# Four input tiles' low parts made ahead of the second projection chunk's low weights, on VectorE

## The chip, the cores and the metric

The kernel runs on one core of a Trainium2 chip. The metric is the device time of one execution in microseconds (us); before the change the median of three runs is 1078.63 us. TensorE multiplies, VectorE (DVE) and ScalarE (ACT) do the elementwise work, and SyncE (SP) issues the transfers from memory.

## The reference

Two transformer blocks over 256 tokens of width 1024, in float32: first an attention block with a gated linear-attention half and a convolved feed-forward part, then a two-layer block (an RWKV-7 layer and a latent-attention layer). Only the start of the first block matters here:

```python
mod = jax.nn.silu(c) @ w_ada[l] + b_ada[l]
shift1, scale1, gate1, shift2, scale2, gate2 = jnp.split(mod, N_MOD, axis=-1)
h = modulate(rms_norm(x, g_norm1[l]), shift1, scale1)      # h * (1 + scale) + shift
proj = h @ w_in[l]                                         # 1024 -> 3088 columns
sb_q, sb_k, sb_v, gq, gk, gv, gg, gf = jnp.split(proj, offsets, axis=-1)
```

`proj` then feeds the stick-breaking attention (`sb_q`, `sb_k`, `sb_v`) and the gated linear attention.

## The kernel before

**Split operands.** Each large product is made in float32 precision from three products of rounded operands. An operand v is split into a high part (v rounded by a copy) and a low part (v minus the high part); then w·x = w_hi·x_hi + w_lo·x_hi + w_hi·x_lo. For weights, ScalarE makes the high part (`act_split`, line 306) and VectorE the low part (`dve_split`, line 321). For the input h of the projection, which lies in SBUF as eight tiles of 128x256 (`kt` 0 to 7), ScalarE makes `h_hi` (line 987), and VectorE scales and shifts the tile in place in `ub` (line 1059) and subtracts (`h_lo`, line 1062).

**Weight stream.** All weights come in chunks of at most 128x2048, in one fixed order, through four buffers (`raw`), issued by SyncE. Before it issues chunk n, SyncE waits until chunk n-4 has been used up: for a split chunk that is VectorE's low part (`lo_made`), for a chunk of `w_ada` it is VectorE's weighted sum (`ada_done`). `w_ada` is not split: ScalarE makes the first two of eight products with c (line 528), VectorE the other six (line 556) and a last sum (line 562), and TensorE sums over the partitions with tiny matmuls (line 572). The order around the change is w_in 0, w_in 2, ada 8, w_in 4, ada 9, w_in 7, ada 10, w_gf, ada 11, w_in 8, ada 12, w_in 9 and so on. With split chunks counted from 0, w_in 0 is chunk 0, w_in 2 chunk 1, w_in 4 chunk 2, w_in 7 chunk 3, w_gf chunk 4 and w_in 8 chunk 5.

**Order of the engines.** Each engine has its own program, written out by hand, and works it off in order; semaphores tie them together. VectorE's program of this part is `dve_one`: after the last `w_ada` chunk of the start it makes the norm's gain (line 1053), then the low weights of chunks 0 and 1 (lines 1055 and 1056), then the eight pairs of lines 1059 and 1062, then `ada` 8 and the low weights of chunk 2, and from there one step for each chunk c: evacuation, an `ada` chunk, a split, and pieces of the attention. ScalarE's program makes the high weights of chunk 0, the eight `h_hi`, the high weights of chunk 1, two copies out of a bank, its part of ada 8, and the high weights of chunk 2; then it waits for the end of chunk 0 on TensorE (line 684).

TensorE multiplies chunks 0 and 1 interleaved (`pe_one`, lines 1181 to 1184). For each chunk a pass of 16 matmuls with each pair of operands:

1. chunk 0: w_hi·h_hi, then w_lo·h_hi
2. chunk 1: w_hi·h_hi, then w_lo·h_hi
3. chunk 0: w_hi·h_lo, then chunk 1: w_hi·h_lo

In step 3 the first matmul that reads tile kt waits for `h_lo` of kt (`wait_h`). After that comes the sum of ada 8, then chunk 2, the sum of ada 9, chunk 3 with the scores of the first pair of attention heads after its second pass (lines 723 to 728), the sum of ada 10, and w_gf. After w_gf comes the second part of the attention pair (line 769). It needs `sW`, which ScalarE makes from the scores in three steps (lines 752, 754 and 756, after the high weights of chunk 5) and VectorE finishes (line 761, after the low weights of chunk 5).

Of the kernel before, what the change touches and what calls it, by code (L numbers as in the profile page):

```python
# [166 lines left out]
def build(nc, A, outs):  # L167
    ctx = ExitStack()
    with ctx:
# [84 lines left out]
        def V(name, j=0, n=1):  # L254
            o, _ = VOFF[name]
            return vec[:, o + j:o + j + n]
# [4 lines left out]
        def bc(ap, n, w):  # L261
            return ap.rearrange("p (a f) -> p a f", a=1).to_broadcast([P, n, w])
# [24 lines left out]
        def by_96(b):  # L287
            return b[:, 0:768].rearrange("p (k c) -> p k c", c=96)

        def by_128(b):  # L290
            return b[:, 0:1024].rearrange("p (k c) -> p k c", c=128)
# [16 lines left out]
        def dve_split(dve, k):  # L308
            if k >= len(split_n):
                return  # L310
            n = split_n[k]
            w = CHUNKS[order[n][0]][1]
            s = k % NSPLIT
            dve.wait_ge(*hi_made.at(k))
            if order[n] in ROTARY:
                for to, of in TWICE:
                    x = dve.tensor_tensor(by_128(lo_s[s])[:, :, to], by_96(raw[n % NRAW])[:, :, of],
                                          by_128(hi_s[s])[:, :, to].bitcast(F), SUB)
                x.then_inc(*lo_made.tick(k))
                return  # L320
            dve.tensor_tensor(lo_s[s][:, 0:w], raw[n % NRAW][:, 0:w], hi_s[s][:, 0:w].bitcast(F),  # L321
                              SUB).then_inc(*lo_made.tick(k))
# [208 lines left out]
        def dve_ada(dve, i):  # L531
            n = at_n["ada", i]
            w = raw[n % NRAW]
            z = [a.rearrange("p a f -> p (a f)") for a in ada_z(i)]
            dve.wait_ge(*d_raw[n % NRAW].at(n))
            if 4 <= i < 8:
                dve.wait_ge(*ada_p.at(i - 4))
            if 10 <= i <= 18:
                dve.wait_ge(*ada_p.at(i - 2))
            if i >= 19:  # L540
                dve.wait_ge(*ada_p.at(i - 1))
            for kt in range(8):
                c = cs[:, kt:kt + 1]
                wk = w[:, kt * 256:kt * 256 + 256]
                if kt < 2:
                    if i in BY_ACT:
                        continue
                    if i == 0:
                        dve.wait_ge(*misc_a.at("cs"))
                    dve.tensor_scalar(z[kt], wk, c, None, MUL).then_inc(*mod_v.tick(("ada", i, kt)))  # L550
                else:
                    if kt < 4 and i in BY_ACT:
                        dve.wait_ge(*mod_a.at(i))
                    else:
                        dve.wait_ge(*mod_v.at(("ada", i, kt - 2)))
                    x = dve.scalar_tensor_tensor(out=z[kt % 2], in0=wk, scalar=c, in1=z[kt % 2], op0=MUL, op1=ADD)  # L556
                    if i in (6, 7) and kt == 7:
                        x.then_inc(*ada_done.tick(i))
                        return
                    x.then_inc(*mod_v.tick(("ada", i, kt)))  # L560
            dve.wait_ge(*mod_v.at(("ada", i, 7)))
            dve.tensor_tensor(z[0], z[0], z[1], ADD).then_inc(*ada_done.tick(i))
# [12 lines left out]
        def dve_mod(dve, o, n, plus, key):  # L575

            dst, src, b = mod[:, o:o + n], mbank[:, o:o + n], V("b_ada", o, n)
            if plus:
                x = dve.scalar_tensor_tensor(out=dst, in0=src, scalar=1.0, in1=b, op0=ADD, op1=ADD)
            else:  # L580
                x = dve.tensor_tensor(dst, src, b, ADD)
            x.then_inc(*mod_v.tick(key))
# [18 lines left out]
        def dve_square8(dve, tag):  # L601
            q = squares[tag]
            dve.wait_ge(*sq_a.at((tag, 1)))
            dve.tensor_tensor(q[:, 0:4, :], q[:, 0:4, :], q[:, 4:8, :], ADD).then_inc(*sq_v.tick((tag, 0)))
            dve.wait_ge(*sq_v.at((tag, 0)))
            dve.tensor_tensor(q[:, 0:2, :], q[:, 0:2, :], q[:, 2:4, :], ADD).then_inc(*sq_v.tick((tag, 1)))
# [12 lines left out]
        def dve_rs_column(dve):  # L619
            dve.wait_ge(*rs_p.at("column"))  # L620
            dve.tensor_copy(rs_c, bank[4][:, 0:2]).then_inc(*misc_v.tick("column"))
# [409 lines left out]
        def dve_one(dve):  # L1031
            dve_ada(dve, 0)
            dve_square8(dve, "mem")
            dve_ada(dve, 1)
            dve_square8(dve, "n1")
            dve_ada(dve, 2)
            dve_rs_column(dve)
            dve_evac1(dve, 0)
            dve_ada(dve, 3)
            dve.wait_ge(*rs_a.at("n1"))  # L1040
            for kt in range(0, 8, 4):
                dve.tensor_tensor(ub[:, kt:kt + 4, :], X[:, kt:kt + 4, :], bc(rs_t[:, :], 4, T),
                                  MUL).then_inc(*ub_v.tick(("n1", kt)))
            dve_ada(dve, 4)
            dve_ada(dve, 5)
            dve_evac1(dve, 2)
            dve_ada(dve, 6)
            dve_ada(dve, 7)
            dve.wait_ge(*ada_p.at(7))
            dve_mod(dve, 8, 8, True, "scale1")  # L1050
            dve_mod(dve, 0, 8, False, "shift1")
            dve.wait_ge(*mod_v.at("scale1"))
            dve.tensor_tensor(mod[:, 8:16], mod[:, 8:16], V("g_norm1", 0, 8), MUL).then_inc(*mod_v.tick("gain1"))
            dve.wait_ge(*mod_v.at("gain1"))
            dve_split(dve, 0)
            dve_split(dve, 1)
            for kt in range(8):
                dve.wait_ge(*h_hi_made.at(("n1", kt)))
                dve.tensor_scalar(ub[:, kt, :], ub[:, kt, :], mod[:, 8 + kt:9 + kt], mod[:, kt:kt + 1], MUL,
                                  ADD).then_inc(*ub_v.tick(("h1", kt)))  # L1060
                dve.wait_ge(*ub_v.at(("h1", kt)))
                dve.tensor_tensor(h_lo[:, kt, :], ub[:, kt, :], h_hi[:, kt, :].bitcast(F),  # L1062
                                  SUB).then_inc(*h_lo_made.tick(("n1", kt)))
            dve_ada(dve, 8)
            dve_split(dve, 2)
            for c in range(NM, N1 + 1):
                if c == 17:
                    dve_mix(dve, 3)
                if c > NM:
                    dve_evac1(dve, c - 1)  # L1070
                if c == 16:
                    dve_gout(dve, 0)
                    dve_mix(dve, 2)
                if c == 17:
                    dve_gout(dve, 1)
                    dve_mix_gla(dve, 1)
                if c == 16:
                    dve.wait_ge(*ada_p.at(17))
                    dve_mod(dve, 16, 8, True, "gate1")
                    dve.wait_ge(*mod_v.at("gate1"))  # L1080
                if NM < c <= 16 and c in ADA_AT:
                    dve_ada(dve, ADA_AT[c])
                if c == 10:
                    dve_mix(dve, 0)
                    dve_scan(dve)
                if c == 11:
                    dve_ktr(dve)
                    dve_kv(dve, 0)
                if c == 12:
                    dve_mix(dve, 1)  # L1090
                    dve_kv(dve, 1)
                if c == 13:
                    dve_go(dve, 0)
                    dve_go(dve, 1)
                if c > NM:
                    dve_split(dve, c - 2)
                if c == 10:
                    dve_kdec(dve)
                if c == 5:
                    dve.wait_ge(*d_con.at(0))  # L1100
                    for n, nm in enumerate(("ident", "nm_su", "zero", "nm_su", "nm_il", "zero", "nm_il")):
                        x = dve.tensor_copy(masks[:, n, :], C(nm))
                    x.then_inc(*misc_v.tick("masks"))
                if c == 7:
                    dve_z(dve, 0)
                if c == 9:
                    dve_gate(dve)
                    dve_z(dve, 1)
                if c == 14:
                    dve_gnorm(dve, 0)  # L1110
                    dve_gnorm(dve, 1)
                    dve_z(dve, 2)
                if c == 15:
                    dve_z(dve, 3)
                if c == 16:
                    dve_mix_gla(dve, 0)
# [2302 lines left out]
```

## Time and profile before

| | |
|---|---|
| median of 3 runs | 1078.63 us (1077.39 to 1078.85) |
| the profiled execution's own time | 1081.68 us |
| its span | 1079.9 us |
| TensorE busy | 1043.6 us, 97% |
| VectorE busy | 734.0 us, 68% |
| ScalarE busy | 562.2 us, 52% |
| mean granted TensorE clock | 0.991 |

The profile is of one execution. Its span is the time from the first to the last recorded instruction; the execution's own time holds 1.78 us more. Times of the trace are counted from the span's start. Matmuls are pipelined and their ends are modelled, so distances between starts of matmuls are safer than their durations. In a row that merges several instructions, the start is that of the first.

### The profile page before, as it was taken

The numbers are of one execution on the slowest core, as the hardware profiler recorded it, in microseconds if no ns is written. First come the engines' busy times: TensorE is split into PE (matmuls) and PEld (weight loads), VectorE is DVE, ScalarE is ACT, GpSimd is POOL, SyncE is SP. The second block draws the span as 40 slices with busy tenths as digits, with TensorE's granted clock in tenths as the row PEclk, the third lists the DMA queues.
The fourth block names the chain that finished last, engine by engine and source line by source line (L and its number), as shares of the span: only waits on it lengthen the run. The fifth ranks groups of instructions, "written<-read, shape, count | busy, mean of one in ns | idle before, by whom it ended". The sixth has DMA issues, their size and how long they took to land.

```text
span 1079.9 us, 22956 instructions
## 1 busy us (share of the span) xinstructions
PE 1043.6 (97%) x9990; PEld 989.0 (92%) x9990; DVE 734.0 (68%) x1194; ACT 562.2 (52%) x858; POOL 0.9 (0%) x7
## 2 busy tenths in 40 slices
PE   7999999999999999998899999999999999999997
PEld 6798898999999998887779999999989799999996
DVE  4798658899976667887547565566757665556554
ACT  4446374655655448754236444454667655444431
POOL 0000000000000000000000000000000000000000
PEclk8999999999999999999999999999999999999999
DMA  9958555466645553331004555356324435554451
GB/s 350 396 216 313 177 192 207 180 220 241 230 138 178 208 225 117 118 119 42 4 2 164 199 187 193 135 188 210 113 74 139 175 136 196 193 182 148 171 166 39
DMA packets 31236, 185.82 MB, mean 172 GB/s; under 512 B 3472, under 2 KB 4768, under 8 KB 13984
## 3 DMA queue, kind: packets, MB, share of 16 engines
q1 hardware_dynamic: 31136, 184.36, 47.8%
q8 instruction: 79, 1.29, 0.5%
q14 instruction: 21, 0.17, 0.0%
HBM read 183.29 MB, written 1.05 MB: 171 GB/s over the span
## 4 chain that ended last, share of the span: by engine, by line
PE 86%; DVE 6%; ACT 3%; DMA 2%; issue 2%; SPq 1%; DVEq 0%; ACTq 0%
PE banks L361 47%; PE banks L1361 17%; PE banks L341 4%; PE banks L358 2%; PE banks L637 2%; DMA land<-in_mkv_a 1%; DVE wlo L321 1%; PE banks L1904 1%; PE banks L1545 1%; ACT whi L306 1%; PE banks L1894 1%; PE banks L572 1%; DMA raw<-in_a_in 1%; DVE adac L556 1%; PE banks L640 1%
## 5 line engine op out<-in xcount | busy, mean ns | idle before, releaser
L321 DVE TENSOR_TENSOR wlo<-raw,whi 128x2048 fp32r<-128x2048 f32 (+3 forms) x163 | 323.1, 1983 | 174.4 <-ACT whi L306 173.8
L306 ACT ACTIVATE whi<-raw 128x2048 fp32r<-128x2048 f32 (+3 forms) x163 | 270.5, 1661 | 110.7 <-PE banks L1361 78.7
L361 PE MATMUL banks<-h_hi,whi 128*128 128x256 f32 x1376 | 180.6, 282 | 1.0 <-ACT h_hi L987 0.3
L361 PE MATMUL banks<-h_lo,whi 128*128 128x256 f32 x1376 | 179.6, 281 | 0.8 <-DVE h_lo L1062 0.8
L361 PE MATMUL banks<-h_hi,wlo 128*128 128x256 f32 x1376 | 177.7, 281 | 0.0
L361 PEld LDWEIGHTS banks<-h_hi,whi 128*128 128x128 f32 x1376 | 168.6, 188 | 4.7 <-ACT h_hi L987 2.1
L361 PEld LDWEIGHTS banks<-h_lo,whi 128*128 128x128 f32 x1376 | 167.7, 187 | 4.2 <-issue 2.6
L361 PEld LDWEIGHTS banks<-h_hi,wlo 128*128 128x128 f32 x1376 | 168.0, 188 | 1.6 <-issue 1.2
L1387 ACT ACTIVATE u<-u 128x256 f32<-128x256 f32 x44 | 18.4, 418 | 128.9 <-DVE u L1441 128.9
L1361 PE MATMUL banks<-m_lo,whi 128*128 128x256 f32 x528 | 75.6, 282 | 0.0
L1361 PE MATMUL banks<-m_hi,whi 128*128 128x256 f32 x528 | 75.5, 281 | 0.0
L1361 PE MATMUL banks<-m_hi,wlo 128*128 128x256 f32 x528 | 75.5, 281 | 0.0
L1361 PEld LDWEIGHTS banks<-m_lo,whi 128*128 128x128 f32 x528 | 68.3, 189 | 0.0
L1361 PEld LDWEIGHTS banks<-m_hi,whi 128*128 128x128 f32 x528 | 68.3, 189 | 0.0
L1361 PEld LDWEIGHTS banks<-m_hi,wlo 128*128 128x128 f32 x528 | 68.3, 189 | 0.0
L1381 ACT ACTIVATE u<-banks,vec 128x256 f32<-128x256 f32 x44 | 22.5, 562 | 49.7 <-PE banks L361 48.3
L385 ACT ACTIVATE ssb<-X 128x256 f32<-128x256 f32 x48 | 19.2, 409 | 41.9 <-DVE X L1472 11.8
L341 PE MATMUL banks<-h_hi,whi 128*128 128x256 f32 x144 | 29.5, 286 | 3.6 <-ACT h_hi L435 1.4
L1458 DVE TENSOR_TENSOR m_lo<-u,m_hi 128x256 fp32r<-128x256 f32 x66 | 27.5, 416 | 4.3 <-ACT m_hi L1397 4.3
L1397 ACT ACTIVATE m_hi<-u 128x256 fp32r<-128x256 f32 x66 | 26.7, 405 | 5.0 <-DVE u L1455 5.0
L556 DVE SCALAR_TENSOR_TENSOR adac<-raw,cs,adac 128x256 f32<-128x256 f32 x66 | 27.1, 479 | 3.3 <-ACT adac L528 3.2
L341 PE MATMUL banks<-h_hi,wlo 128*128 128x256 f32 x144 | 28.6, 279 | 0.0
(449 smaller groups left out, 1405.8 us busy)
## 6 DMA issues: line engine op xcount, KB each, us to landing
raw<-in_ada SPq DMA_DIRECT2D x24, 1024.0 KB, 5.7
raw<-in_w_up SPq DMA_DIRECT2D x22, 1024.0 KB, 4.8
raw<-in_a_gu SPq DMA_DIRECT2D x22, 1024.0 KB, 4.8
raw<-in_b_gu SPq DMA_DIRECT2D x22, 1024.0 KB, 4.9
raw<-in_w_in SPq DMA_DIRECT2D x12, 1024.0 KB, 6.3
raw<-in_w_down SPq DMA_DIRECT2D x16, 704.0 KB, 4.1
raw<-in_a_in SPq DMA_DIRECT2D x11, 1024.0 KB, 5.0
raw<-in_a_down SPq DMA_DIRECT2D x16, 704.0 KB, 4.1
```

What stands on the lines that cost most here:

```text
L306: act.activation(hi_s[k % NSPLIT][:, 0:w], raw[n % NRAW][:, 0:w], ACT.Copy).then_inc(*hi_made.tick(k))
L321: dve.tensor_tensor(lo_s[s][:, 0:w], raw[n % NRAW][:, 0:w], hi_s[s][:, 0:w].bitcast(F), SUB).then_inc(*lo_made.tick(k))
L341: i_ = pe.matmul(b[0:m, j * T:(j + 1) * T], a[:, kt * step + j * m:kt * step + j * m + m], x[:, kt, :], start=o == 0 and j == 0, stop=sp)
L358: i_ = pe.matmul(b[:, j * m:(j + 1) * m], x[:, kt, j * P:j * P + P], a[:, kt * step:kt * step + m], start=st, stop=sp)
L361: i_ = pe.matmul(b[0:m, j * T:(j + 1) * T], a[:, kt * step + j * m:kt * step + j * m + m], x[:, kt, :], start=st, stop=sp)
L385: act.activation(ssb[:, j, :], src, ACT.Square).then_inc(*sq_a.tick((tag, kt)))
L556: x = dve.scalar_tensor_tensor(out=z[kt % 2], in0=wk, scalar=c, in1=z[kt % 2], op0=MUL, op1=ADD)
L637: x = pe.matmul(b[:, j * T:j * T + T], mem_g[:, kt, j * P:j * P + P], w[:, kt * T:kt * T + T], start=o == 0, stop=o == 15)
L1361: x_ = pe.matmul(b[:, 0:T], a[:, kt * P:kt * P + P], x[:, 11 * half + kt, :], start=half == 0 and o == 0, stop=half == 1 and last)
L1381: act.activation(z[:, j, :], b[:, j * T:j * T + T], ACT.Identity, bias=V("b_conv", f), scale=V("w_conv2", f)).then_inc(*up_a.tick((tag, "t ...
L1397: act.activation(m_hi[:, i - 2, :], u[(i - 2) % NU][:, 0, :], ACT.Copy).then_inc(*m_hi_a.tick((tag, i - 2)))
L1458: dve.tensor_tensor(m_lo[:, i - 2, :], u[(i - 2) % NU][:, 0, :], m_hi[:, i - 2, :].bitcast(F), SUB).then_inc(*m_lo_v.tick((tag, i - 2)))
```

## The change

VectorE makes the low parts of the tiles kt 0 to 3 directly after the low weights of chunk 0; the low weights of chunk 1 come behind them, and the tiles kt 4 to 7 behind those. No instruction is added or removed, and the other engines' programs stay as they are.

```diff
--- before.py
+++ after.py
@@ -1053,8 +1053,9 @@
             dve.tensor_tensor(mod[:, 8:16], mod[:, 8:16], V("g_norm1", 0, 8), MUL).then_inc(*mod_v.tick("gain1"))
             dve.wait_ge(*mod_v.at("gain1"))
             dve_split(dve, 0)
-            dve_split(dve, 1)
             for kt in range(8):
+                if kt == 4:
+                    dve_split(dve, 1)
                 dve.wait_ge(*h_hi_made.at(("n1", kt)))
                 dve.tensor_scalar(ub[:, kt, :], ub[:, kt, :], mod[:, 8 + kt:9 + kt], mod[:, kt:kt + 1], MUL,
                                   ADD).then_inc(*ub_v.tick(("h1", kt)))
```

## Rows read from the trace of the kernel before

**Rows 1.** The page: busy share of TensorE and its number of instructions.

```profile
PE 1043.6 (97%) x9990; PEld 989.0 (92%) x9990; DVE 734.0 (68%) x1194; ACT 562.2 (52%) x858; POOL 0.9 (0%) x7
```

**Rows 2.** Waits, 36 to 75 us: engine, line, waited for: us in total, times, longest.

```profile
DVE wlo L321 <- ACT whi L306: 3.7, 1, 3.7
...
PE banks L361 <- DVE h_lo L1062: 0.8, 2, 0.4
```

**Rows 3.** VectorE in order of time, 49 to 86 us: start, us, what, idle before.

```profile
49.57 2.29 DVE L321 TENSOR_TENSOR wlo<-raw,whi 128x2048 fp32r<-128x2048 f32 x1
55.52 2.29 DVE L321 TENSOR_TENSOR wlo<-raw,whi 128x2048 fp32r<-128x2048 f32 x1 [3.66 <-ACT whi L306]
57.73 0.41 DVE L1059 TENSOR_SCALAR ub<-ub,mod 128x256 f32<-128x256 f32 x1
...
60.87 0.41 DVE L1059 TENSOR_SCALAR ub<-ub,mod 128x256 f32<-128x256 f32 x1
...
64.01 2.46 DVE L556 SCALAR_TENSOR_TENSOR adac<-raw,cs,adac 128x256 f32<-128x256 f32 x6
...
69.05 2.46 DVE L556 SCALAR_TENSOR_TENSOR ssb<-raw,cs,ssb 128x256 f32<-128x256 f32 x6
...
82.79 2.29 DVE L321 TENSOR_TENSOR wlo<-raw,whi 128x2048 fp32r<-128x2048 f32 x1 [1.79 <-ACT whi L306]
85.24 0.96 DVE L761 SCALAR_TENSOR_TENSOR sW<-banks,sW 128x768 f32<-128x768 f32 x1 [0.16 <-ACT sW L756]
```

**Rows 4.** ScalarE in order of time, 49 to 83 us.

```profile
49.63 4.05 ACT L987 ACTIVATE h_hi<-ub,mod 128x256 fp32r<-128x256 f32 x8 [2.51 <-DVE mod L1053]
53.59 1.90 ACT L306 ACTIVATE whi<-raw 128x2048 fp32r<-128x2048 f32 x1
...
65.52 0.60 ACT L684 ACTIVATE land<-banks 128x512 f32<-128x512 f32 x1 [6.71 <-PE banks L361]
66.02 0.90 ACT L528 ACTIVATE ssb<-raw,cs 128x256 f32<-128x256 f32 x2
...
80.83 1.92 ACT L306 ACTIVATE whi<-raw 128x2048 fp32r<-128x2048 f32 x1 [3.02 <-DMA raw<-in_w_in]
```

**Rows 5.** TensorE in order of time, 60 to 87 us.

```profile
60.18 2.03 PE L361 MATMUL banks<-h_hi,wlo 128*128 128x256 f32 x16
62.04 0.93 PE L361 MATMUL banks<-h_lo,whi 128*128 128x256 f32 x6
63.37 0.39 PE L361 MATMUL banks<-h_lo,whi 128*128 128x256 f32 x1 [0.40 <-DVE h_lo L1062]
64.15 3.22 PE L361 MATMUL banks<-h_lo,whi 128*128 128x256 f32 x25 [0.40 <-DVE h_lo L1062]
67.21 0.50 PE L572 MATMUL banks<-one,adac 128*128 128x1 f32 x4
...
69.55 2.05 PE L358 MATMUL banks<-wlo,h_hi 128*128 128x256 f32 x16
72.02 0.61 PE L572 MATMUL banks<-one,ssb 128*128 128x1 f32 x4 [0.42 <-DVE ssb L562]
...
86.25 0.91 PE L769 MATMUL banks<-sW,con 128*128 128x384 f32 x2 [1.33 <-DVE sW L761]
```

**Rows 6.** The chain of waits, 50 to 90 us, in order of time: start, us, what.

```profile
71.97 2.21 DVE wlo L321
...
74.20 6.61 DMA raw<-in_w_in
```

**Rows 7.** ScalarE's line 987 alone: duration ns min/median/max, first and last start.

```profile
L987 ACT ACTIVATE h_hi<-ub,mod x8: 583/586/600, 49.6 to 53.1; 128x256 fp32r<-128x256 f32 x8
```

**Rows 8.** SyncE's issues in order of time.

```profile
66.96 0.33 SPq L280 DMA_DIRECT2D raw<-in_ada  x1
```

**Rows 9.** Two stretches: us, busy of PE, PEld, DVE, ACT, POOL, granted clock, DMA share, GB/s.

```profile
52.00:56.00 4.00, 3.57 (x15) 2.83 (x15) 0.48 (x1) 4.00 (x7) 0.00 (x0) 0.74 0.91 338
504.00:508.00 4.00, 3.89 (x47) 3.47 (x48) 0.86 (x2) 1.51 (x2) 0.00 (x0) 0.57 0.00 0
```

## The prediction

> **What bounds the kernel now.** The page comes first. TensorE is busy 97% of the span [rows 1], so a gain can only be a hole of TensorE that closes, and every other engine counts by what it makes TensorE wait for. So I read the waits of the stretch around the change. VectorE stands idle 3.7 us for one thing, ScalarE's high weights of chunk 1, while TensorE waits 0.8 us in two pieces for `h_lo` [rows 2]. The timelines say why. VectorE ends the low weights of chunk 0 about 51.8 us, holds until 55.52 us, and makes the eight pairs of `ub` and `h_lo` only then, from 57.73 to 64.01 us [rows 3]. Their own inputs had long been there: ScalarE's eight `h_hi` start at 49.63 us and are over before 53.7 us [rows 4]. TensorE comes to its `h_lo` passes at 62.04 us, ahead of the last tiles [rows 5].
>
> The second thing to see is that this delay is handed on. From 55.52 us VectorE has no idle time until 82.79 us [rows 3], and SyncE issues when VectorE releases a buffer. The low weights of chunk 3 end at 74.18 us, SyncE then issues w_in 8, it lands 6.61 us later [rows 6], ScalarE has waited 3.02 us for it [rows 4], and behind its high weights come `sW` and a TensorE hole of 1.33 us that ends at 86.25 us [rows 5]. VectorE, through SyncE, sets the end of this stretch, not TensorE.
>
> **The change, part by part.** *What moves on VectorE.* A pair of lines 1059 and 1062 costs (60.87 - 57.73)/4 = 0.785 us from start to start, four cost 3.14 us [rows 3]. A split costs 57.73 - 55.52 = 2.21 us until the next can start, so the moved pairs can begin at 49.57 + 2.21 = 51.78 us and would be over at 54.92 us [rows 3]. Tile 3 needs its `h_hi`: those come every (53.59 - 49.63)/8 = 0.495 us [rows 4] and last 0.586 us [rows 7], so the fourth is there at 49.63 + 3 x 0.495 + 0.586 = 51.70 us. No pair waits. The low weights of chunk 1 still start at 55.52 us, when ScalarE has made the high ones; the hole that hides the pairs is 55.52 - 51.78 = 3.74 us, and 0.60 us of it stays. Were it gone, each further us would delay chunk 1's low weights, with tiles 4 to 7, ada 8 and all later steps of VectorE queued behind, and SyncE's issue of w_in 7; the gain would shrink by as much. The instruction moved past them adds no wait of its own to anything that was earlier.
>
> *The new neighbour.* VectorE now writes tiles 0 to 3 of `ub` in place while ScalarE still reads tiles 4 to 7. The trace has no row of just this. The nearest: the eight `h_hi` of ScalarE, of which the first ran beside VectorE's split and the last beside an idle VectorE, take 583 to 600 ns [rows 7]. If the last four took the longest of these instead of the shortest, that is 4 x 0.017 = 0.07 us; no row speaks for a gain. I take 0 and keep 0.07 us.
>
> *What comes earlier.* Tiles 4 to 7 are made from 57.73 to 60.87 us, over 1 us ahead of TensorE's first `h_lo` pass at 62.04 us. Ada 8 on VectorE begins at 64.01 - 3.14 = 60.87 us. VectorE has been busy without a gap, so everything behind moves by 3.14 us if its inputs do. The one that is close is ada 9, which needs ScalarE's two products. ScalarE's order before them is a copy of chunk 0's bank, which waits for TensorE.
>
> *TensorE.* A pass of 16 takes 62.04 - 60.18 = 1.86 us, two take 3.72 us. The `h_lo` passes took 67.21 - 62.04 = 5.17 us [rows 5]. Without waits they end 1.45 us earlier; the sum of ada 8 is ready by then (it moves by 3.14 us). Chunk 0's own pass ended its 16 matmuls at 64.15 + 9 x 0.116 = 65.20 us and would end them at 62.04 + 1.86 = 63.90 us, so ScalarE's copy moves by 1.30 us, from 65.52 to 64.22 us [rows 4, 5]. Its products for ada 9 were ready at 66.02 + 0.90 = 66.92 us, now 65.62 us; VectorE comes to them at 69.05 - 3.14 = 65.91 us. That fits by 0.29 us. Then TensorE's wait of 0.42 us for the sum of ada 9 goes too (VectorE 3.14 us earlier, TensorE 1.45). TensorE alone is now 1.87 us earlier.
>
> *SyncE and the transfers.* The split of chunk 1 releases its buffer when it did, so w_in 7 is issued as before. Ada 10, issued at 66.96 us on VectorE's end of ada 8 [rows 8], and all behind it in SyncE's queue come 3.14 us earlier in the same distances from each other: w_in 8 at 71.06 us, landing at 77.67 us instead of 80.81 us [rows 6]. ScalarE had been free since 80.83 - 3.02 = 77.81 us, and what it did before waited for transfers that move as well. So its high weights start at 77.7 us, VectorE's low ones follow, and `sW`, ready at 85.24 + 0.96 = 86.20 us, is ready at 83.06 us.
>
> *The sum.* TensorE came to line 769 at 86.25 - 1.33 = 84.92 us; it now comes at 84.92 - 1.87 = 83.05 us and finds `sW` at 83.06 us. Of the 1.33 us some 0.1 us at most is left. Line 769 starts at 86.25 - 3.14 = 83.11 us. What ends last is still VectorE's queue, so the gain is its 3.14 us and not the 1.45 us of the wait in view. At this point TensorE, VectorE, ScalarE and SyncE all stand 3.14 us earlier, and no later step depends on anything but these, so the shift goes through to the end. In the profiled execution 1081.68 - 3.14 = 1078.54 us (span 1079.9 to 1076.8). That execution is 3.05 us above the median of the runs; from the median it is 1078.63 - 3.14 = 1075.49 us.
>
> **The rivals.** *A, the transfer doesn't come earlier.* If w_in 8 landed at 80.8 us whatever its issue, TensorE would win 1.87 us and lose it again in the hole before line 769: 1078.6 us. For it: the landing is what ScalarE waits for longest here, and 6.61 us is long. Against: three transfers that it could queue behind move with it. *B, ScalarE is late with ada 9.* The margin is 0.29 us. If ScalarE did not move at all, VectorE would start ada 9 at 66.92 instead of 65.91 us, and of 3.14 us 2.13 us would stay: 1076.5 us. Against: TensorE's pass has no other wait.
>
> *C, the clock, and the slower side.* TensorE's granted clock fell to its lower level, 1.2 of 2.4 GHz, after the thin matmuls of 50 to 54 us, and again after a pause at 503 us; 504 to 508 us stand at 0.57 [rows 9]. That is 4 x (1 - 0.57)/0.5 = 3.4 us at the lower level, 1.7 us of work lost. If the shift brings one more such stretch, 1.7 of 3.14 us are gone: 1077.2 us. From two on it is no faster, and for slower by more than the bound it takes (3.14 + 2.16)/1.7, so four: 1075.5 + 6.8 = 1082.3 us. For it: the same kernel's runs lie 1.46 us apart, and the profiled one 3 us above. Against: the change closes TensorE's pauses and opens none, and the drop at 54 us lies before it. If the stretch at 504 us fell away it would be 1073.8 us. The Trainium skill (TensorE: Matmul & The Clock Gate, Part 1: The HAM clock gate) says that the monitor's window runs free and isn't set to a kernel's start. By that rule a moved stretch can win or lose one such drop by chance alone, which is case C with one stretch either way; one trace can't show it.
>
> **How the numbers follow.** What a measurement of this kernel can tell from no change is 0.2%, 2.16 us: faster means below 1076.47 us. My forecast with all of 3.14 us: 0.76, its own range 1074.7 to 1076.4 us (the 0.07 us above, and half of the runs' 1.46 us either way). One low-clock stretch fewer: 0.04. B, or one more stretch: 0.09. A: 0.07. Four more stretches: 0.04. So faster 0.80, the same 0.09 + 0.07 = 0.16, slower 0.04. The range goes from 1073.8 us (one stretch fewer) to 1077.4 us (B, and one stretch more, within a little); A and the slower case stay out with 0.11.
>
> **What would show it.** In the profile after: VectorE's idle time before chunk 1's low weights is 0.6 us instead of 3.66, and these still start near 55.5 us; ScalarE's `h_hi` still take 0.59 us; TensorE has no wait for `h_lo` and its sum of ada 8 starts near 65.8 us; ada 9 on VectorE starts near 65.9 us without idle time; w_in 8 is issued near 71.1 us and lands near 77.7 us; line 769 starts near 83.1 us with 0.2 us of idle time or less. The prediction is wrong if the landing of w_in 8 stays near 80.8 us (A), if VectorE idles before ada 9 (B), if line 769 is 3.1 us earlier and the span is not (C), or if chunk 1's low weights start after 55.6 us.

## The result, and the profile after

The changed kernel takes 1075.51 us (median of 7 runs, 1073.61 to 1076.03), the kernel before 1078.05 us beside it (7 runs, 1076.47 to 1079.09). The ratio is 0.997, with a 95% interval of 0.9957 to 0.9983: faster, by 2.5 us in the medians. The forecast was 1075.5 us. Timed once more, the ratio was 0.9979 (0.9965 to 0.9993), 1075.98 against 1078.61 us.

The profiled execution has a span of 1072.5 us against 1079.9 us. That is 7.4 us, far more than the medians differ, so only part of it can be the change. I compare places, and count from the start of chunk 0's low weights on VectorE, the last step before the change takes hold: 49.57 us before [rows 3], 49.27 us after.

VectorE after, in order of time (start, us, what, idle before it):

```profile
49.27 2.29 DVE L321 TENSOR_TENSOR wlo<-raw,whi 128x2048 fp32r<-128x2048 f32 x1
...
51.48 0.41 DVE L1060 TENSOR_SCALAR ub<-ub,mod 128x256 f32<-128x256 f32 x1
...
55.21 2.29 DVE L321 TENSOR_TENSOR wlo<-raw,whi 128x2048 fp32r<-128x2048 f32 x1 [0.52 <-ACT whi L306]
...
57.42 0.41 DVE L1060 TENSOR_SCALAR ub<-ub,mod 128x256 f32<-128x256 f32 x1
...
60.57 2.46 DVE L556 SCALAR_TENSOR_TENSOR adac<-raw,cs,adac 128x256 f32<-128x256 f32 x6
...
65.60 2.46 DVE L556 SCALAR_TENSOR_TENSOR ssb<-raw,cs,ssb 128x256 f32<-128x256 f32 x6
...
79.37 2.29 DVE L321 TENSOR_TENSOR wlo<-raw,whi 128x2048 fp32r<-128x2048 f32 x1 [1.83 <-ACT whi L306]
...
81.82 0.96 DVE L761 SCALAR_TENSOR_TENSOR sW<-banks,sW 128x768 f32<-128x768 f32 x1 [0.16 <-ACT sW L756]
```

These answer to [rows 3]. The hole in front of chunk 1's low weights has shrunk from 3.66 to 0.52 us; the four pairs lie in it, from 51.48 us. Chunk 1's low weights are 5.94 us behind chunk 0's (5.95 before): the moved work cost them nothing. Ada 8 follows at 60.57 us, 11.30 us behind the start of chunk 0's low weights instead of 14.44 us: 3.14 us earlier. Ada 9 starts at 65.60 us with no idle time before it.

ScalarE after:

```profile
49.33 4.05 ACT L987 ACTIVATE h_hi<-ub,mod 128x256 fp32r<-128x256 f32 x8 [2.54 <-DVE mod L1053]
...
53.28 1.90 ACT L306 ACTIVATE whi<-raw 128x2048 fp32r<-128x2048 f32 x1
...
63.80 0.60 ACT L684 ACTIVATE land<-banks 128x512 f32<-128x512 f32 x1 [5.30 <-PE banks L361]
...
64.30 0.90 ACT L528 ACTIVATE ssb<-raw,cs 128x256 f32<-128x256 f32 x2
...
77.42 1.92 ACT L306 ACTIVATE whi<-raw 128x2048 fp32r<-128x2048 f32 x1 [2.98 <-DMA raw<-in_w_in]
```

Against [rows 4], its eight `h_hi` take 4.05 us as before, although VectorE now writes other tiles of the same buffer beside them. Its two products for ada 9 end at 64.30 + 0.90 = 65.20 us, 0.40 us ahead of VectorE.

TensorE after:

```profile
59.87 2.03 PE L361 MATMUL banks<-h_hi,wlo 128*128 128x256 f32 x16
...
61.74 3.90 PE L361 MATMUL banks<-h_lo,whi 128*128 128x256 f32 x32
...
65.47 0.50 PE L572 MATMUL banks<-one,adac 128*128 128x1 f32 x4
...
67.81 2.06 PE L358 MATMUL banks<-wlo,h_hi 128*128 128x256 f32 x16
...
69.70 0.50 PE L572 MATMUL banks<-one,ssb 128*128 128x1 f32 x4
...
81.39 1.09 PE L361 MATMUL banks<-h_lo,whi 128*16 128x256 f32 x8
82.83 0.91 PE L769 MATMUL banks<-sW,con 128*128 128x384 f32 x2 [0.35 <-DVE sW L761]
```

The `h_lo` passes are one row of 32 matmuls without a wait, 65.47 - 61.74 = 3.73 us instead of 5.17 us in [rows 5]. The sum of ada 9 has no wait either. Line 769 starts at 82.83 us with 0.35 us of idle time instead of 1.33 us; from chunk 0's low weights it is 33.56 us instead of 86.25 - 49.57 = 36.68 us. That is 3.12 us.

The chain and SyncE's issue, after, answering to [rows 6, 8]:

```profile
68.52 2.21 DVE wlo L321
...
70.75 6.65 DMA raw<-in_w_in
```

```profile
63.51 0.33 SPq L280 DMA_DIRECT2D raw<-in_ada  x1
```

Ada 10 is issued at 63.51 instead of 66.96 us, w_in 8 at 70.75 instead of 74.20 us, and it takes 6.65 us to land (6.61 before). Less the 0.30 us by which the executions differ at the start, each is 3.15 us earlier.

The clock, answering to [rows 9]; columns as there:

```profile
52.00:56.00 4.00, 3.67 (x15) 3.08 (x16) 3.38 (x8) 4.00 (x7) 0.00 (x0) 0.68 0.89 307
504.00:508.00 4.00, 3.49 (x120) 2.69 (x112) 3.96 (x6) 1.08 (x2) 0.00 (x0) 1.00 0.00 0
```

The stretch at TensorE's lower level behind the thin matmuls of 50 to 54 us is there as before. That at 504 us is missing. This (about 1.5 us, by the starts of VectorE's low weights on either side of it) and something slower that piles up between 224 and 405 us (1.75 us) make up most of the rest of the 7.4 us. The experiments below show that both come and go with the execution.

### The profile page after: what moved, and what is told of

Read it like the earlier page. It is cut to its first block, busy times and chain, and to the rows that moved or that the text cites. A ratio compares the mean times of both kernels' runs of the same rounds, so it can differ in the third digit from the quotient of the medians.

```text
span 1072.5 us, 22956 instructions
## 1 busy us (share of the span) xinstructions
PE 1038.6 (97%) x9990; PEld 985.2 (92%) x9990; DVE 733.8 (68%) x1194; ACT 562.0 (52%) x858; POOL 0.9 (0%) x7
## 4 chain that ended last, share of the span: by engine, by line
PE 88%; DVE 5%; ACT 3%; DMA 2%; issue 1%; SPq 1%; DVEq 0%; ACTq 0%
PE banks L361 48%; PE banks L1362 17%; PE banks L341 5%; PE banks L358 2%; PE banks L637 2%; DVE wlo L321 1%; DMA land<-in_mkv_a 1%; PE banks L1546 1%; PE banks L1905 1%; PE banks L1895 1%; PE banks L572 1%; DVE adac L556 1%; PE banks L640 1%; PE banks L1911 1%; DMA raw<-in_w_in 1%
```

## The experiments

Theory V: what is gained is time in VectorE's queue. Work moves into a hole, and all that VectorE releases later, through SyncE's transfer of w_in 8 and `sW` up to line 769, comes earlier by as much. Theory T: what is gained is TensorE's wait for `h_lo`, the wait in view.

**The queue filled up again.** The early tiles stay; VectorE does the same amount of other work behind tile 7.

```diff
+        pad = sb("pad", [P, 4, T], F, sc)
...
+            for kt in range(4):
+                dve.tensor_scalar(pad[:, kt, :], X[:, kt, :], mod[:, 8:9], mod[:, 0:1], MUL,
+                                  ADD).then_inc(*ub_v.tick(("pad", kt)))
+                dve.wait_ge(*ub_v.at(("pad", kt)))
+                dve.tensor_tensor(pad[:, kt, :], pad[:, kt, :], X[:, kt, :], SUB).then_inc(*ub_v.tick(("pad2", kt)))
             dve_ada(dve, 8)
```

Expected: 

> The changed kernel, with four more pairs of VectorE operations of the size of a tile pair (on a scratch tile, results unused) behind tile 7's low part and ahead of ada 8. Theory V (VectorE's queue is what is gained, 3.14 us): TensorE still has no wait for h_lo, but ada 8 on VectorE starts near 63.7 us instead of 60.57, line 769 near 86.0 us instead of 82.83, with about 3 us of idle time before it, and the time is that of the kernel before, 1078.1 us (ratio 1.000). Theory T (what is gained is TensorE's wait for h_lo): the extra operations cost nothing, 1.5 to 1.9 us of the gain stay, 1076.4 us.

Measured: 1080.32 us against 1080.15 us, ratio 1.000 (0.9985 to 1.0015). TensorE in this kernel:

```profile
62.04 3.89 PE L361 MATMUL banks<-h_lo,whi 128*128 128x256 f32 x32
...
67.02 0.61 PE L573 MATMUL banks<-one,adac 128*128 128x1 f32 x4 [1.09 <-DVE adac L563]
...
72.06 0.61 PE L573 MATMUL banks<-one,ssb 128*128 128x1 f32 x4 [0.54 <-DVE ssb L563]
...
85.64 0.91 PE L770 MATMUL banks<-sW,con 128*128 128x384 f32 x2 [0.68 <-DVE sW L762]
```

TensorE has its 32 `h_lo` matmuls without a wait, as theory T wants, and the gain is gone. The saved wait has turned into 1.09 us before the sum of ada 8 and 0.54 us before that of ada 9. Theory T falls by these rows; in time its forecast (1076.4 of 1078.1 us, a ratio of 0.9985) lies just on the edge of the interval. Line 769 is 36.02 us behind the start (49.62 us), where 36.68 us was forecast. The whole difference lies in one transfer: w_in 8 was issued 24.62 us behind the start, as before (24.63 us), but ScalarE could use it 5.98 us later instead of 6.63 us. The idle time right before line 769 is 0.68 us and not the forecast 3 us, for the same reason and because I had left out that TensorE loses its lead already in the two earlier waits.

**Two tiles instead of four.**

```diff
-                if kt == 4:
+                if kt == 2:
                     dve_split(dve, 1)
```

Expected: 

> Two tiles' low parts instead of four ahead of chunk 1's low weights. Theory V: the gain is what fits in VectorE's hole, so it is halved: VectorE's idle time before chunk 1's low weights 2.1 us, line 769 near 84.4 us (82.83 + 1.57), time 1077.1 us. Theory T: tile 7 is ready at 61.9 us, before TensorE reads it at 62.6 us, so TensorE has no wait for h_lo and the whole gain stays: 1075.5 us, line 769 near 82.8 us.

Measured: 1079.13 us against 1080.15 us, ratio 0.9991 (0.9977 to 1.0005). VectorE and TensorE in this kernel:

```profile
56.26 2.29 DVE L321 TENSOR_TENSOR wlo<-raw,whi 128x2048 fp32r<-128x2048 f32 x1 [2.09 <-ACT whi L306]
...
63.19 2.46 DVE L556 SCALAR_TENSOR_TENSOR adac<-raw,cs,adac 128x256 f32<-128x256 f32 x6
```

```profile
62.79 3.90 PE L361 MATMUL banks<-h_lo,whi 128*128 128x256 f32 x32
...
85.41 0.91 PE L769 MATMUL banks<-sW,con 128*128 128x384 f32 x2 [1.33 <-DVE sW L761]
```

Again 32 `h_lo` matmuls without a wait, but line 769 is 85.41 - 50.31 = 35.10 us behind the start: 1.58 us earlier than before, half of the 3.12 us, with the hole half filled (2.09 us left). In time the interval holds no change and the forecast half gain (1077.1 us, a ratio of 0.9991), and theory T's whole gain (0.9976) lies only just outside it; the rows decide, not the time.

**All eight tiles.**

```diff
             dve_split(dve, 0)
             for kt in range(8):
-                if kt == 4:
-                    dve_split(dve, 1)
...
+            dve_split(dve, 1)
             dve_ada(dve, 8)
```

Expected: 

> All eight tiles' low parts ahead of chunk 1's low weights. Theory V: the hole held 3.74 us, so only 0.6 us more of work fits; chunk 1's low weights start near 57.8 us instead of 55.21 and ada 8 near 60.0 us instead of 60.57. TensorE waits about 0.2 us for chunk 1's low weights near 59.9 us; w_in 7 is issued 2.55 us later (60.1 us). Line 769 between 82.5 and 83.1 us, time 1075.3 to 1075.8 us. If each tile ahead brought 0.785 us as the first four did, it would be 1072.4 us.

Measured: 1076.49 us against 1080.15 us, ratio 0.9972 (0.996 to 0.9985), not to be told from the 0.997 with four tiles. The rival by which each tile brings 0.785 us (1072.4 us, a ratio of 0.9948) is outside the interval. VectorE and TensorE:

```profile
57.92 2.29 DVE L321 TENSOR_TENSOR wlo<-raw,whi 128x2048 fp32r<-128x2048 f32 x1
...
60.12 2.46 DVE L556 SCALAR_TENSOR_TENSOR adac<-raw,cs,adac 128x256 f32<-128x256 f32 x6
...
65.80 2.46 DVE L556 SCALAR_TENSOR_TENSOR ssb<-raw,cs,ssb 128x256 f32<-128x256 f32 x6 [0.55 <-ACT ssb L528]
```

```profile
60.26 2.14 PE L361 MATMUL banks<-h_hi,wlo 128*128 128x256 f32 x16 [0.20 <-DVE wlo L321]
...
82.83 0.87 PE L769 MATMUL banks<-sW,con 128*128 128x384 f32 x2
```

The hole is full and more: TensorE waits 0.20 us for chunk 1's low weights, ada 8 comes 60.12 - 49.44 = 10.68 us behind the start (11.30 with four tiles), and then VectorE idles 0.55 us before ada 9, for ScalarE's products. That is rival B's mechanism, which four tiles just miss. Line 769 ends up at 33.39 us, without idle time: here TensorE itself is last.

**Five tiles.**

```diff
-                if kt == 4:
+                if kt == 5:
                     dve_split(dve, 1)
```

Expected: 

> Five tiles' low parts instead of four ahead of chunk 1's low weights. Theory V: the fifth pair (0.785 us) takes the 0.52 us that VectorE still idles and 0.26 us more; chunk 1's low weights start 0.2 to 0.3 us later, ada 8 0.5 us earlier. TensorE comes to line 769 when it did and had idled 0.35 us there, so that line moves by 0.2 to 0.35 us, to 33.2 to 33.4 us behind the start of chunk 0's low weights (33.56 with four). In time nothing that can be told from four: 1075.2 us, ratio 0.997. A rival by which each further tile ahead brings 0.785 us: 1074.7 us.

Measured: 1075.83 us against 1079.39 us, ratio 0.9963 (0.9946 to 0.9979).

```profile
55.51 2.28 DVE L321 TENSOR_TENSOR wlo<-raw,whi 128x2048 fp32r<-128x2048 f32 x1
...
65.42 2.47 DVE L556 SCALAR_TENSOR_TENSOR ssb<-raw,cs,ssb 128x256 f32<-128x256 f32 x6 [0.23 <-ACT ssb L528]
```

```profile
81.50 1.09 PE L361 MATMUL banks<-h_lo,whi 128*16 128x256 f32 x8
82.44 0.89 PE L769 MATMUL banks<-sW,con 128*128 128x384 f32 x2
```

VectorE has no hole left before chunk 1's low weights, and 0.23 us before ada 9. Line 769 is 82.44 - 49.38 = 33.06 us behind the start, 0.50 us less than with four tiles, where 0.2 to 0.35 us was expected. The transfer of w_in 8 was 0.2 us shorter here. And TensorE had more room than the 0.35 us of idle time, which are counted from a modelled end: the last row before line 769 starts 32.12 us behind the start in both kernels (81.39 - 49.27 and 81.50 - 49.38), and without a wait line 769 follows it by 0.94 us here, with four tiles by 1.44 us. The room was 0.50 us. The time can't be told from that with four.

**TensorE made faster instead.** TensorE multiplies chunk 0's low weights between the high ones while the `h_hi` arrive.

```diff
+        MIXED = [(0, 0), (0, 1), (0, 2), (0, 3), (1, 0), (0, 4), (1, 1), (0, 5), (1, 2), (0, 6), (1, 3), (0, 7),
+                 (1, 4), (1, 5), (1, 6), (1, 7)] + [(2, kt) for kt in range(8)]
...
-                                (name, i) in TOK1, wait_h("n1") if c < NM + 2 else None)
+                                (name, i) in TOK1, wait_h("n1") if c < NM + 2 else None,
+                                MIXED if c == NM else ())
...
-            for g, times in ((0, 4), (1, 4), (0, 2), (1, 2)):
+            for g, times in ((0, 2), (1, 4), (0, 1), (1, 2)):
```

Expected: 

> The changed kernel, with TensorE multiplying chunk 0's low weights tile by tile between the high ones while ScalarE still makes h_hi (the same 64 matmuls before the h_lo passes, in another order). Chunk 1's first pass should start near 55.2 us instead of 58.00 and the h_lo passes end near 63.5 us instead of 65.47, and the stretch at TensorE's lower clock near 54 us should go or shrink. Theory V: VectorE and SyncE stay where they are, so line 769 stays at 82.8 us (not more than 0.35 us earlier) with about 2.3 us of idle time before it, time 1075.2 to 1075.5 us. Theory T: TensorE is the bound and all 2 us come through, 1073.5 us.

Measured: 1076.22 us against 1080.15 us, ratio 0.9969 (0.995 to 0.9988), not to be told from the changed kernel's 0.997. But theory T's 1073.5 us (a ratio of 0.9958) is inside this interval too, so the rows have to decide. The clock and TensorE:

```profile
52.00:56.00 4.00, 3.40 (x26) 3.19 (x26) 3.35 (x10) 4.00 (x7) 0.00 (x0) 1.00 0.90 352
```

```profile
56.48 2.14 PE L361 MATMUL banks<-h_hi,whi 128*128 128x256 f32 x16 [1.08 <-ACT mvB L683]
...
64.06 0.60 PE L574 MATMUL banks<-one,adac 128*128 128x1 f32 x4
...
69.10 0.61 PE L574 MATMUL banks<-one,ssb 128*128 128x1 f32 x4 [0.54 <-DVE ssb L564]
...
83.32 0.91 PE L771 MATMUL banks<-sW,con 128*128 128x384 f32 x2 [1.33 <-DVE sW L763]
```

The clock stays at its upper level (1.00 where it was 0.68), and the `h_lo` passes end at 64.06 - 49.79 = 14.27 us behind the start instead of 16.20 us. All of these 1.93 us are given back. By starts, 0.81 us are gone by the sum of ada 9 (5.04 us behind that of ada 8 instead of 4.23 us; it now has 0.54 us of idle time), and 1.09 us more by line 769 (14.22 instead of 13.13 us; 1.33 us of idle time), which is at 33.53 us, where it was (33.56 us). The mirror image of the first experiment: TensorE faster, VectorE's queue unchanged, nothing gained. Two points were off. The idle time before line 769 was forecast at 2.3 us; part of it came before the sum of ada 9 instead. And chunk 1's first pass began 6.69 us behind the start (56.48 us) instead of 5.93 us, because it needs a bank that ScalarE copies out behind chunk 1's high weights (line 681 in the kernel before), a wait that had been covered.

**Both together**, five tiles and TensorE's new order.

Expected: 

> Five tiles first, and TensorE's order of dense_first_chunk. Theory V: neither brings much alone, because line 769 needs both TensorE and sW; together TensorE is 1.5 us or more ahead and VectorE's queue is 0.5 us ahead, so line 769 moves by the queue's 0.5 us, to 33.0 us behind the start of chunk 0's low weights, and idle time of 1 us or more stays before it: 1074.9 us, ratio 0.9965 to 0.997. Theory T (TensorE is the bound) has 2.3 us more than the changed kernel: 1073.2 us.

Measured: 1074.79 us against 1079.39 us, ratio 0.9956 (0.994 to 0.9972); line 769 at 84.01 - 51.13 = 32.88 us behind the start, 0.68 us earlier than in the changed kernel. It was then timed beside the changed kernel.

Expected of the changed kernel: 

> The changed kernel, unchanged, timed on the same chip as the next one, to set the two side by side: ratio to the kernel before 0.997, line 769 33.4 to 33.6 us behind the start of chunk 0's low weights.

Expected of the combination: 

> Five tiles first with TensorE's tile order of dense_first_chunk, timed once more. Theory V: line 769 is 0.5 to 0.7 us earlier than in the changed kernel; in addition the lower-clock stretch near 54 us is gone, but its cost had been hidden ahead of line 769, so it brings nothing more. Ratio to the kernel before 0.9965 and to the changed kernel 0.9994, which five rounds hardly tell from 1. If the vanished low-clock stretch or TensorE's lead counted, it would be 2 us faster than the changed kernel, 0.998.

Measured on one chip: the changed kernel 1075.98 us, ratio 0.9979 (0.9965 to 0.9993), line 769 at 33.39 us behind the start (51.01 us); the combination 1074.61 us, ratio 0.9971 (0.9956 to 0.9985), line 769 at 33.05 us:

```profile
82.58 0.91 PE L771 MATMUL banks<-sW,con 128*128 128x384 f32 x2 [1.48 <-DVE sW L763]
```

1.48 us of idle time stay before line 769, so TensorE's lead is unused, as theory V has it. The combination had the lower median here, the one time that the two stood side by side (1074.61/1075.98 = 0.9987, between the forecasts of 0.9994 and 0.998), but the intervals overlap widely: that it is faster than the changed kernel is likely from its rows (0.3 to 0.7 us) and not shown by its time.

The changed kernel's profile holds one thing more that bears on the two theories. The low-clock stretch near 54 us is missing in it, although nothing in the kernel differs:

```profile
52.00:56.00 4.00, 3.30 (x14) 1.94 (x14) 3.88 (x8) 4.00 (x8) 0.00 (x0) 1.00 0.93 352
```

```profile
61.94 3.89 PE L361 MATMUL banks<-h_lo,whi 128*128 128x256 f32 x32
...
84.40 0.91 PE L769 MATMUL banks<-sW,con 128*128 128x384 f32 x2 [1.18 <-DVE sW L761]
```

TensorE begins its `h_lo` passes 61.94 - 51.01 = 10.93 us behind the start instead of 12.47 us, 1.54 us earlier, and line 769 is where it was, with 1.18 us of idle time before it. So the low-clock stretch ahead of line 769 costs the changed kernel nothing, and of the 1.93 us that TensorE won in the kernel with the denser order, about 1.5 us can be the clock alone. That the denser order is what keeps the clock up is likely but not shown: all three profiles with that order are without the stretch, and of the nine others this one alone is.

**The two kernels profiled again**, to see what of the 7.4 us belongs to the execution.

Expected of the kernel before: 

> The kernel before, unchanged, profiled once more. If the part of the two spans' difference (7.4 us) that lies behind line 769 belongs to the execution and not to the change, this profile has line 769 again 36.7 us behind the start of chunk 0's low weights on VectorE (49.57 to 86.25 us in the first), but its later stretches differ from the first profile's: the stretch at TensorE's lower clock near 504 us is elsewhere or missing, and the 1.7 us that 230 to 430 us took longer than in the changed kernel may be gone. If they belong to the kernel before, both are there again.

Expected of the changed one: 

> The changed kernel, unchanged, profiled once more: line 769 again 33.6 us behind the start of chunk 0's low weights. If the rest belongs to the execution, the span is likely longer than 1072.5 us, toward 1073.7 us and more.

Measured: spans 1076.2 and 1074.8 us, line 769 at 86.73 - 50.52 = 36.21 us and 82.92 - 49.51 = 33.41 us behind the start. The kernel before:

```profile
86.73 0.91 PE L769 MATMUL banks<-sW,con 128*128 128x384 f32 x2 [0.87 <-DVE sW L761]
```

```profile
504.00:508.00 4.00, 4.00 (x107) 3.60 (x108) 0.90 (x3) 2.54 (x3) 0.00 (x0) 1.00 0.00 0
```

The changed kernel:

```profile
500.00:504.00 4.00, 2.65 (x12) 2.42 (x12) 1.77 (x4) 0.67 (x1) 0.00 (x0) 0.61 0.01 4
```

The low-clock stretch near 504 us has changed sides: the kernel before is without it this time, the changed one has it (at 501 us). In its first two profiles the kernel before differs from itself by 3.7 us of span, the changed kernel by 2.3 us. What stays in all profiles is the part ahead of line 769: 36.2 and 36.7 us before, 33.4 to 33.6 us after (three profiles).

## Why the prediction was right

*VectorE's hole and the moved pairs.* Forecast: four pairs for 3.14 us, fitting in 3.74 us, 0.60 us left. Measured: ada 8 3.14 us earlier, 0.52 us left. Two, five and eight tiles give 1.58, 3.62 and 3.29 us at line 769, against 3.12 us with four: the gain grows with what fits in the hole and stops there. The last three lie close together, since line 769 moves by some 0.5 us with the transfer of w_in 8 alone.

*The new neighbour.* Taken at 0, with 0.07 us kept; ScalarE's eight tiles take 4.05 us as before.

*TensorE's own part.* Forecast 1.87 us earlier at line 769; measured: it came there at 82.83 - 0.35 = 82.48 us, 33.21 us behind the start against 35.35 us, so 2.14 us. The term was 0.27 us too small, mostly because I took the wait for ada 9's sum from its idle time (0.42 us) instead of from the distances of starts: 72.02 - 69.55 = 2.47 us [rows 5] against 69.70 - 67.81 = 1.89 us, which makes 0.58 us. It changed nothing, since `sW` comes last.

*SyncE, the transfer, and the sum.* Forecast 3.14 us at the issue of w_in 8, at its landing, and at line 769. The issue moved by 3.13 to 3.15 us between any two profiles of the two kernels. Line 769 moved by 3.12 us between the first two profiles, and by 2.6 to 3.3 us between any two, as the time from the issue to ScalarE's use varies from one execution to the next. That the gain is VectorE's 3.14 us and not the 1.45 us in view is shown from both sides, by the refilled queue and by the denser first chunk.

*To the end.* Forecast: nothing behind line 769 takes it back. The medians moved by 2.54 and 2.63 us, and 3.14 us is inside both intervals (0.9957 to 0.9983 is 1.8 to 4.6 us). The rows follow the shift for 140 us: the low weights that VectorE starts at 227.67 us before and 224.22 us after are 3.15 us nearer to the start in the first two profiles, and in the second two (228.09 and 224.30 us) 2.78 us, where line 769 had moved by 2.80 us. Behind that the executions differ by more than the change is worth. Whether the missing half microsecond is anything but scatter stays open. That the forecast time, 1075.5 us, was met to within 0.1 us is luck in part: the gain in the medians came out 0.6 us smaller than forecast, and the kernel before, timed beside it, 0.6 us faster than the 1078.63 us from which the forecast was counted.

*The rivals.* A (the landing doesn't move) is refuted by the row of 70.75 us: w_in 8 lands at 77.40 us. B (ScalarE late with ada 9) had 0.40 us of margin instead of 0.29, as ScalarE's products moved by 1.42 us instead of 1.30; it is real, and shows with five and eight tiles. C (the clock) is real as scatter: one such stretch came and went in both kernels. Its price of 1.7 us holds for a stretch like that at 504 us; one ahead of line 769 cost nothing there, as the profile without the stretch near 54 us shows. The Trainium skill (TensorE: Matmul & The Clock Gate, Part 1: The HAM clock gate) says that the clock's monitor runs free of the kernel's start, and the profiles fit that: the kernel before has 504 to 508 us at 0.57 in one execution and at 1.00 in another, and the changed kernel 52 to 56 us at 0.68 in one and at 1.00 in another.

## What to carry to other kernels

A wait that holds an engine's queue (here for another engine's output) costs what is queued behind it; look for later work whose inputs are already there and that fits the hole, and no more of it than fits. The gain is then to be read where that queue's releases end last, several transfers later, not at the wait that vanishes. To test such a reading, refill the queue behind the moved work, and speed up the engine that seemed to wait: neither takes more than a few lines.

## What the runs showed that was not expected

Two profiles of one execution each differed by 7.4 us of span where the medians differ by 2.5 us. Beside the low-clock stretch, TensorE worked at one of two rates in the dense stretch of the first feed-forward part, with the same granted clock in the records. The first profile of before, and then of after (PE's matmuls are the first count):

```profile
276.00:296.00 20.00, 20.00 (x172) 20.00 (x172) 18.37 (x35) 12.90 (x19) 0.00 (x0) 1.00 0.61 225
```

```profile
276.00:296.00 20.00, 20.00 (x174) 20.00 (x173) 18.72 (x35) 11.80 (x18) 0.00 (x0) 1.00 0.60 201
```

The counts of a fixed stretch depend a little on where it cuts; distances between two fixed points tell more. From the low weights that VectorE starts at 257.25 us after (260.88 us before) to those at 325.63 us (329.84 us), TensorE does 584 matmuls without idle time. This takes 68.38 us in the first profile of after and 68.96 us in that of before, 117.1 against 118.1 ns for each. The changed kernel's second profile has the slower rate:

```profile
257.73 2.29 DVE L321 TENSOR_TENSOR wlo<-raw,whi 128x2048 fp32r<-128x2048 f32 x1
...
326.69 1.63 DVE L321 TENSOR_TENSOR wlo<-raw,whi 128x1408 fp32r<-128x1408 f32 x1 [0.85 <-ACT whi L306]
```

That is 68.96 us again. Of the twelve profiles seven take 68.38 or 68.39 us and five 68.96 us, and none lies between. It isn't the change: the kernel before is slow in both its profiles, but the changed one is fast in two and slow in one, the kernel with the refilled queue, which takes as long as the kernel before, has the faster rate, and that with the dense first chunk, as fast as the changed one, the slower. What sets it stays open. Between 224 and 405 us the kernel before took 1.75 us longer than the changed one in the first two profiles, and the changed kernel's second profile 2.37 us longer than its first. A single profile of this kernel can therefore mislead by more than the change is worth, while the distance of line 769 from the start of chunk 0's low weights repeats to 0.5 us, and VectorE's steps up to ada 9 to 0.02 us. TensorE's own steps ahead of line 769 do not repeat that well: they moved by 1.54 us with the clock.

Also, w_in 8, a transfer of 1 MB, was usable by ScalarE 5.98 to 6.75 us after its issue in the twelve profiles, and that alone was most of what differed between executions of one kernel up to line 769.
